# A hybrid encoder layer: attention by kv group with wide moving value products, and half of the out projection between its heads

## The chip, the cores and the metric

The kernel runs on one core of a Trainium2 chip. The metric is the device time of one execution in microseconds (us); lower is better. The engines of the core work side by side, each through its own list of instructions in order, and wait for one another by semaphores: TensorE (PE in the profile) multiplies, VectorE (DVE), ScalarE (ACT) and GpSimd (POOL) do the rest, and SyncE (SP) issues most transfers.

## The reference

One layer is applied to two sequences with shared weights, 1024 and 256 tokens, of width 1024. Cut to what matters:

```
h = rms_norm(x); q, k, v, z, xbc, dt, mq = split(h @ w_in)
q = rope(rms_norm(q))                       # 16 heads of 64
k = rope(rms_norm(k))                       # 4 kv heads, each shared by 4 query heads
for each block of 128 queries, with its 3 neighbouring key blocks:
    sc = q k^T * scale, masked to |i - j| <= 128 and to the sequence
    m = max(max(sc), sink); p = exp(sc - m); denom = sum(p) + exp(sink - m)
    attn = (p / denom) @ v
ssm_out = bidirectional state-space scan; mem_out = attention to 256 memory tokens
x = x + concat(attn, ssm_out, mem_out) @ w_out      # 2048 x 1024
x = x + W_down(silu(conv(gate)) * conv(up)),  [gate, up] = rms_norm(x) @ w_up
```

All is float32. Where precision allows, the kernel splits an operand into a high part in a reduced form (F32R) and a low rest, and multiplies in two or three passes.

## The kernel before

The 1280 tokens are 10 tiles of 128 (`NT`): 8 of the long sequence (`TP`) and 2 of the short. The stages follow one another, each a block with its own buffers and semaphores: norm, input projections, ssm, `attention`, `memory`, `out_projection`, `ffn`. Between stages the data lies in DRAM: `proj` holds the projections, `mix_t` the concatenated outputs, turned, a tile at a time as 128 x (16 x 128).

**`attention`** first prepares all keys (norm, rotary, turned into `kt_hi` and `kt_lo`, with zero blocks at the ends of each sequence), and then loops over tiles and in each over 16 heads (`tile`). A head takes two score products over 384 columns (L969, L970) into `s_ps`, a custom VectorE operation that masks, scales and takes the maximum (L887, `at_sm`, `at_nm`), the exponential on ScalarE (L752, `at_pr`), three turns of the weights on TensorE (L943, `at_tps`), a VectorE copy (L867, `at_pt`), and the value product (L955), in which a block of 128 weights is the stationary operand and 64 value columns are the moving one, in float32:

```python
for k in range(3):
    m = T.matmul(o_ps[:, h], pt[:, h % 2, k], rhs, start=(k == 0), stop=(k == 2))
```

The steps of a head are spread over the slots of the next heads: turns two heads late, values four. Queries of the next tile are prepared on GpSimd in operations of 128 x 1024 (L672 to L686), `high` on ScalarE (L716) stands in head 4 and the turns (`q_unit`, L922) in heads 10 to 13, into two banks of `x_ps` by turns, evacuated by ScalarE (L720). The outputs are divided by the denominator (L852), turned (`o_unit`, L935) and stored.

**`memory`** is the same kind of attention over 256 memory tokens.

**`out_projection`** multiplies `mix_t` by the 16 row chunks of `w_out` in two parts, of 10 and 6 chunks, since not all split weights fit beside the result: the first part for all tiles, then the second, each adding into `x1` in SBUF. A chunk is three products of 512 columns for each half of the width. Loads of the mix go from ScalarE's queue. In the second part each tile is also normed, turned (`turn`) and split into `h_hi` and `h_lo` for the ffn. Lines: splits of the weights on VectorE L2028 and L2030, of the mix L1975 (ScalarE) and L2042 (VectorE), products L2141 and L2120.

**`ffn`** holds `x1` in SBUF and adds to it.

In every stage the order of work on each engine is written out by hand.

## Time and profile before

| | |
|---|---|
| device time, 3 runs | 2328.8, 2332.81 (median), 2338.07 us |
| span of the profiled execution, first to last instruction | 2327.3 us |
| own time of that execution beside its span | not recorded; the median of the runs is 5.5 us above the span |
| attention, first transfer to the next stage's first | 710.5 to 1022.4 us |
| memory | 1022.4 to 1119.8 us |
| out projection | 1119.8 to 1374.8 us |
| ffn | 1374.8 us to the end |

The profile is one execution, recorded by the hardware. Durations of matmuls overlap with those of the next (their ends are modelled), so how fast TensorE works is read from the distance between the starts of two instructions. `[x <-y]` behind a row is the idle time of the engine before it, and what ended it. `x4` is a row in which four like instructions are merged.

### The profile page before, as it was taken

To read this page: it belongs to the slowest core of one execution; us is meant where nothing else is said; L and a number is where in the kernel's file an instruction comes from. 1 tells how busy PE (TensorE), PEld (TensorE's weight loads), DVE (VectorE), ACT (ScalarE), POOL (GpSimd) and SP (SyncE) were. 2 spreads that over 40 slices of the span, in tenths; PEclk is the share of its full clock that TensorE was granted. 3 is DMA by queue.
4 is the path that set the end of the run, shared out by engine and by line. 5 is a ranking of instruction groups with operands and counts; after the bars stand their busy time and mean duration, and the time that the engine had idled before them with its cause. 6 is when DMAs were issued, how large, how long until landed. Compare 5 with 4: busy or idle time off the path is not lost. (4 is left out here: it accounts for less than half of the span.)

```text
span 2327.3 us, 30823 instructions
## 1 busy us (share of the span) xinstructions
PE 2098.8 (90%) x10912; PEld 1759.7 (76%) x10912; DVE 1366.6 (59%) x1843; ACT 609.6 (26%) x1163; POOL 295.5 (13%) x239
## 2 busy tenths in 40 slices
PE   4999999987862899958699979999999999999997
PEld 3887888865652888957578868888888888888885
DVE  6562211116976788857432545667667576676766
ACT  5111111103652656635110322211212112111110
POOL 2000000003654655413000000000000000000000
PEclk7999999999985999979899989999999999999998
DMA  5322222223212111111541121110101101001002
GB/s 169 106 82 84 83 85 87 97 81 105 73 50 101 35 44 43 43 72 60 192 153 43 41 64 45 49 34 27 54 27 33 48 27 54 27 27 54 27 9 90
DMA packets 109191, 152.57 MB, mean 66 GB/s; under 512 B 8512, under 2 KB 68928, under 8 KB 109120
## 3 DMA queue, kind: packets, MB, share of 16 engines
q1 hardware_dynamic: 82784, 109.74, 15.1%
q10 hardware_dynamic: 26336, 41.89, 5.1%
q8 instruction: 44, 0.72, 0.1%
q14 instruction: 27, 0.22, 0.0%
HBM read 115.43 MB, written 36.18 MB: 65 GB/s over the span
## 5 line engine op out<-in xcount | busy, mean ns | idle before, releaser
L2350 DVE TENSOR_TENSOR x<-x,ff_proj 128x512 f32<-128x512 f32 x264 | 181.5, 688 | 190.5 <-PE ff_proj L2411 188.3
L2391 PE MATMUL ff_proj<-h_hi,ff_uhi 128*128 128x512 f32 (+1 forms) x1056 | 264.3, 358 | 10.4 <-DVE ff_ulo L2304 10.4
L2391 PE MATMUL ff_proj<-h_lo,ff_uhi 128*128 128x512 f32 (+1 forms) x1056 | 263.6, 358 | 0.0
L2391 PE MATMUL ff_proj<-h_hi,ff_ulo 128*128 128x512 f32 (+1 forms) x1056 | 263.3, 358 | 0.0
L2391 PEld LDWEIGHTS ff_proj<-h_hi,ff_uhi 128*128 128x128 f32 x1056 | 177.2, 188 | 43.1 <-DVE ff_ulo L2304 10.8
L2391 PEld LDWEIGHTS ff_proj<-h_lo,ff_uhi 128*128 128x128 f32 x1056 | 175.5, 188 | 31.2
L2391 PEld LDWEIGHTS ff_proj<-h_hi,ff_ulo 128*128 128x128 f32 x1056 | 175.5, 188 | 31.3
L416 PE MATMUL pj_bank<-pj_whi,act_hi 128*128 128x512 f32 x464 | 180.7, 390 | 0.0
L416 PE MATMUL pj_bank<-pj_whi,act_lo 128*128 128x512 f32 x464 | 180.5, 389 | 0.0
L416 PE MATMUL pj_bank<-pj_wlo,act_hi 128*128 128x512 f32 x464 | 180.5, 389 | 0.0
L327 DVE CAST pj_whi<-pj_raw 128x1024 fp32r<-128x1024 f32 x36 | 24.9, 692 | 206.1 <-PE pj_bank L416 179.2
L955 PEld LDWEIGHTS at_ops<-at_v,at_pt 128*128 128x128 f32 x960 | 127.3, 191 | 19.9 <-DVE at_pt L867 19.5
L2262 ACT ACTIVATE ff_padded<-ff_proj 128x1024 f32<-128x1024 f32 x44 | 45.3, 1029 | 361.7 <-PE ff_proj L2391 361.7
L955 PE MATMUL at_ops<-at_v,at_pt 128*128 (+1 forms) x960 | 127.0, 268 | 12.0 <-DVE at_pt L867 11.9
L2274 ACT ACTIVATE ff_ahi<-ff_gate 128x1281 fp32r<-128x1281 f32 x22 | 28.1, 1276 | 381.0 <-DVE ff_gate L2339 381.0
L2350 DVE TENSOR_TENSOR x<-x,ff_sums 128x512 f32<-128x512 f32 x176 | 121.0, 688 | 2.8 <-PE ff_sums L2411 0.8
L752 ACT ACTIVATE at_pr<-at_sm,at_nm 128x384 f32<-128x384 f32 x160 | 98.1, 613 | 85.3 <-DVE at_nm L887 76.6
L2411 PE MATMUL ff_proj<-ff_dhi,ff_ahi 128*128 128x512 f32 x264 | 105.2, 398 | 9.2 <-DVE ff_alo L2341 9.2
L887 DVE CUSTOM_DVE_ANT_0 at_sm<-at_sps,at_mask,at_nsink 128x384 f32<-128x384 f32 x160 | 98.0, 613 | 20.8 <-PE at_sps L970 12.9
L500 ACT ACTIVATE pj_stage<-pj_bank 128x512 f32<-128x512 f32 x58 | 34.7, 598 | 277.5 <-PE pj_bank L416 277.5
L2411 PE MATMUL ff_proj<-ff_dlo,ff_ahi 128*128 128x512 f32 x264 | 104.9, 397 | 0.0
L2411 PE MATMUL ff_proj<-ff_dhi,ff_alo 128*128 128x512 f32 x264 | 104.5, 396 | 0.0
(285 smaller groups left out, 4256.5 us busy)
## 6 DMA issues: line engine op xcount, KB each, us to landing
ff_rawu<-w_up SPq DMA_DIRECT2D x44, 512.0 KB, 5.0
pj_raw<-w_in SPq DMA_DIRECT2D x28, 512.0 KB, 3.9
scratch_proj<-pj_stage ACTq DMA_DIRECT2D x50, 256.0 KB, 2.0
ff_rawd<-w_down SPq DMA_DIRECT2D x22, 512.0 KB, 3.5
wo_raw<-w_out SPq DMA_DIRECT2D x16, 512.0 KB, 4.2
n_x<-tokens SPq DMA_DIRECT2D x14, 512.0 KB, 4.2
wo_mix<-scratch_mix ACTq DMA_DIRECT2D x9, 640.0 KB, 3.8
sb_xc<-scratch_xbc_tiles SPq DMA_DIRECT2D x10, 512.0 KB, 3.3
```

The costliest lines, as they stand in the source:

```text
L327: v.tensor_copy(w_hi[:, s, k], raw[:, q % RAW]).then_inc(w_hi_done, 1)
L416: m = nc.tensor.matmul(out, left(a, k), right(c, k), start=(k == 0 and i == 0), stop=(k == KC - 1 and i == 2))
L500: a.activation(stage[:, s], bank[:, g % BANKS], func).then_inc(copied, 1)
L752: nc.scalar.activation(pr[:, h % 4], sm[:, h % 4], ACT.Exp, bias=nm[:, s, h:h + 1], scale=-1.0, accum_out=rowsum[:, s, h:h + 1]).then_inc( ...
L887: v.tensor_tensor_reduce(out=sm[:, h % 4], in0=s_ps[:, h % 2, 0:WIN], in1=mask[:, s], scale=-(DH ** -0.5), scalar=nsink[:, h:h + 1], op0=A ...
L955: m = T.matmul(o_ps[:, h], pt[:, h % 2, k], rhs, start=(k == 0), stop=(k == 2))
L2262: nc.scalar.activation(padded[:, 1:1 + SEQ], proj[:, g, 0:SEQ], ACT.Copy)
L2274: nc.scalar.activation(a_hi[:, 1:GAP + 1 + DEC], gate[:, 1:GAP + 1 + DEC], ACT.Copy).then_inc(a_hi_done, 1)
L2350: nc.vector.tensor_tensor(v, v, ring(g), ALU.add).then_inc(added, 1)
L2391: m = nc.tensor.matmul(proj[:, g, t0:t0 + n], U[w][:, s, k, g], X[x][:, k, t0:t0 + n], start=(k == 0 and r == 0), stop=(k == KC - 1 and r ...
L2411: m = nc.tensor.matmul(ring(g), a[:, c0:c0 + P], w[:, s, cols], start=(r == 0), stop=(r == 2))
```

## The change

`memory` now runs before `attention`, and `attention` does half of the out projection.

**Order of attention.** The loop runs over the 4 kv groups, in each over the 10 tiles, and in each tile over the group's 4 heads (`slots()`, 160 slots; a unit `u` is a tile of a group). The keys of a group are prepared one group ahead on GpSimd (`keys`), in buffers of two groups, without zero blocks: `blocks(t)` gives the 2 or 3 key blocks that exist, so a tile at an end of a sequence has 256 score columns. Queries are prepared by pairs of tiles, 4 heads each (128 x 512), and turned in two goes, `query_turn(v, 0)` and `(v, 1)`. All turns but those of the weights go through one bank, `x_ps`, in an order that `x_order()` lists.

**Value products.** Values are split and doubled, `v_two` holds a block as [high, low] side by side: 128 columns, the stationary operand. The moving operand is the turned weights of all 4 heads, 512 columns, themselves split into `p_hi` (ScalarE) and `p_lo` (VectorE). So the result is turned already, but has a high and a low half of 64 partitions each, which are stored apart in `mix_t` and `mix_b` and added later, and isn't yet divided: the reciprocals go to DRAM (`rec`), and the next stage multiplies by them.

**Half of the out projection.** Chunks 8 to 15 of `w_out` (the ssm and memory rows) are split in the start of `attention`; tile 0 is multiplied there, and the other 144 chunks one in each slot (`fill`), with the residual added and stored to `part`. The stage `out_projection` does chunks 0 to 7, starting from `part`; a tile's mix is two loads, eight small broadcast loads of the reciprocals, an addition on GpSimd (`whole`) and a multiplication on VectorE (`weigh`). `x1` goes through DRAM and the ffn loads it.

The diff, cut to its core (`...` where lines are left out). TensorE's loop in `attention`:

```diff
+            def rest_of_part():
+
+                for q in range(2, TILE_GROUPS):
+                    n, c = divmod(q, 2)
+                    pe.wait_ge(m_split, n + 1)
+                    pe.wait_ge(added, q - 1)
+                    for k in range(CH):
+                        chunk(n, c, k)
+                        yield
...
+            def x_free(n):
+
+                if n > 0:
+                    pe.wait_ge(S["xcopy"], n)
...
+            def query_turn(v, i):
+                x_free(use_no[("q", v, i)])
+                pe.wait_ge(S["qlo"], v + 1)
+                for h in range(QG):
+                    o = T.transpose(x_ps[:, h], q_two[:, i, h].rearrange("p a d -> p (a d)"), ident[:, :])
+                o.then_inc(S["x"], 1)
...
+            def output(u, x):
...
+                w = v_two[:, g % 2, ks[x]].rearrange("p a d -> p (a d)")
+                T.matmul(o_ps[:, :], w, p_hi[:, c % 2], start=(x == 0), stop=False)
+                T.matmul(o_ps[:, :], w, p_lo[:, c % 2], start=False, stop=(x == len(ks) - 1)).then_inc(S["o"], 1)
...
+            fill = rest_of_part()
+            for u, g, t, h, v in slots():
+                scores(u, g, t, h, v)
+                if h > 0 and u > 0 and h - 1 < len(blocks((u - 1) % NT)):
+                    probs_turn(u - 1, h - 1)
+                if t % 2 == 1 and h < 2 and v + 1 < HKV * PAIRS:
+                    query_turn(v + 1, h)
+                next(fill, None)
+                if h == 3 and u > 0:
+                    output(u - 1, 0)
+                if h < 2 and u > 1 and h + 1 < len(blocks((u - 2) % NT)):
+                    output(u - 2, h + 1)
+                if (t, h) in K_TURN and g + 1 < HKV:
+                    key_turn(g + 1, K_TURN[t, h])
```

ScalarE's and VectorE's loops, and GpSimd's last query step:

```diff
+            for u, g, t, h, v in slots():
+                i, n = t % 2, split_due(QG * u + h)
+                probs(u, h)
+                if h > 0 and u > 0 and h - 1 < len(blocks((u - 1) % NT)):
+                    probs_high(turns_before(u - 1) + h - 1)
+                if n is not None:
+                    mix_high(n)
+                if i == 1 and h == 2 and v + 2 < HKV * PAIRS:
+                    square(v + 2)
+                if i == 0 and h == 3 and v + 1 < HKV * PAIRS:
+                    high(v + 1)
+                if i == 1 and h in (1, 2) and v + 1 < HKV * PAIRS:
+                    query_evac(v + 1, h - 1)
...
+            for u, g, t, h, v in slots():
+                k = QG * u + h
+                scores(u, g, t, h)
+                if h >= 2 and u > 0:
+                    probs_low(turns_before(u - 1) + h - 2)
...
+                if h == 2 and u >= 2:
+                    out_evac(u - 2)
+                n, q = split_due(k), evac_due(k)
+                if n is not None:
+                    mix_low(n)
+                if q is not None and q >= 2:
+                    add(q)
...
+            def queries_low(v):
+                pool.wait_ge(S["qhi"], v + 1)
+                g_.tensor_tensor(q_two[:, :, :, 1].bitcast(F32R), q_c[:, :, :, :], q_two[:, :, :, 0],
+                                 ALU.subtract).then_inc(S["qlo"], 1)
```

`out_projection`, SP's loads and the order of VectorE:

```diff
+            def mixed(t):
+                if t > 0:
+
+                    sp.wait_ge(m_split, t)
+                sp.dma_start(mix[:, :, :], mix_t[t][:, 0:CH * P]).then_inc(mix_loaded, 16)
+                sp.dma_start(mix2[:, :, :], mix_b[t]).then_inc(mix_loaded, 16)
+                for e in range(2):
+                    for g in range(HKV):
+                        sp.dma_start(rec[e * DH:(e + 1) * DH, 2 * g:2 * g + 2],
+                                     rec_v[t, e, g].unsqueeze(0).broadcast_to([DH, 2, P])).then_inc(mix_loaded, 16)
...
+            for t in range(2, NT):
+                mixed(t)
+                store(t - 2)
+                residual(t)
...
+            for t in range(2, NT):
+                weigh(t)
+                add(t - 2)
+                low(t)
+                if t >= 3:
+                    norm(t - 3)
+                    turned(t - 3)
```

The ffn:

```diff
+            load(1)
+            sp.dma_start(y[:, :, :], x1_dram.rearrange("(t p) d -> p t d", p=P)).then_inc(y_loaded, 16)
```

## Rows read from the trace of the kernel before

**Rows 1.** The page: span, and busy time of each engine.
```profile
span 2327.3 us, 30823 instructions
...
PE 2098.8 (90%) x10912; PEld 1759.7 (76%) x10912; DVE 1366.6 (59%) x1843; ACT 609.6 (26%) x1163; POOL 295.5 (13%) x239
```

**Rows 2.** Stretches: us, busy time of engines, PEclk, DMA share, GB/s.
```profile
710.50:758.90 48.40, 9.76 (x57) 8.32 (x57) 34.57 (x36) 14.35 (x20) 30.74 (x15) 0.58 0.32 110
758.90:1013.00 254.10, 238.22 (x1942) 227.23 (x1943) 218.85 (x560) 154.21 (x408) 127.78 (x70) 1.00 0.12 40
1013.00:1022.40 9.40, 5.24 (x44) 4.62 (x43) 3.44 (x10) 2.48 (x7) 0.00 (x0) 0.90 0.14 56
1022.40:1119.80 97.40, 65.37 (x416) 55.30 (x416) 57.31 (x106) 39.82 (x116) 30.34 (x36) 0.85 0.24 78
1119.80:1374.80 255.00, 232.46 (x1040) 190.41 (x1040) 109.08 (x102) 42.98 (x50) 7.46 (x22) 0.96 0.28 95
1119.80:1163.90 44.10, 31.40 (x120) 23.79 (x120) 24.61 (x24) 3.82 (x3) 0.13 (x2) 0.81 0.68 231
```

**Rows 3.** Order of time, head loop: start, us, engine, line, operation.
```profile
847.21 0.60 ACT L752 ACTIVATE at_pr<-at_sm,at_nm 128x384 f32<-128x384 f32 x1
...
847.81 0.60 ACT L752 ACTIVATE at_pr<-at_sm,at_nm 128x384 f32<-128x384 f32 x1
...
848.69 0.42 PE L969 MATMUL at_sps<-at_kthi,at_qt 128*128 x1
...
849.14 0.78 PE L955 MATMUL at_ops<-at_v,at_pt 128*128 x6
849.53 0.62 DVE L887 CUSTOM_DVE_ANT_0 at_sm<-at_sps,at_mask,at_nsink 128x384 f32<-128x384 f32 x1 [0.43 <-PE at_sps L970]
...
849.75 0.50 PE L943 MATMUL at_tps<-at_ident,at_pr 128*128 128x128 f32 x3
...
850.01 0.42 PE L969 MATMUL at_sps<-at_kthi,at_qt 128*128 x1
...
850.07 2.33 DVE L861 TENSOR_TENSOR at_t<-at_nm,at_sink 128x8 f32<-128x8 f32 x1
...
850.19 0.62 ACT L752 ACTIVATE at_pr<-at_sm,at_nm 128x384 f32<-128x384 f32 x1 [0.58 <-DVE at_nm L887]
```

**Rows 4.** Order of time: handovers of queries; in brackets the idle time before.
```profile
757.73 1.09 ACT L720 ACTIVATE at_qt<-at_xps 128x512 fp32r<-128x512 f32 x2 [0.26 <-PE at_xps L922]
...
758.87 0.45 PE L969 MATMUL at_sps<-at_kthi,at_qt 128*128 128x384 f32 x1 [0.69 <-ACT at_qt L720]
...
846.25 1.06 ACT L716 ACTIVATE at_qtwo<-at_qn 128x1024 fp32r<-128x1024 f32 x1 [1.63 <-POOL at_qn L683]
...
847.38 2.37 POOL L686 TENSOR_TENSOR at_qtwo<-at_qn,at_qtwo 128x1024 fp32r<-128x1024 f32 x1 [1.25 <-ACT at_qtwo L716]
```

**Rows 5.** Out projection: two products in order of time; a group of VectorE.
```profile
1164.51 0.39 PE L2120 MATMUL wo_bank<-h_hi,wo_mlo 128*128 128x512 f32 x1
...
1164.74 0.39 PE L2120 MATMUL wo_bank<-h_hi,wo_mhi 128*128 128x512 f32 x1
...
L2030 DVE TENSOR_TENSOR h_lo<-wo_raw,h_hi 128x1024 fp32r<-128x1024 f32 x10 | 12.2, 1224 | 0.3
```

**Rows 6.** The ssm stage: products behind two idle times; a stretch at the second.
```profile
577.54 1.98 PE L1628 MATMUL sf_dps<-sf_atri,sf_ones 128*128 128x512 f32 x4 [2.39 <-POOL sf_atri L1680]
...
644.44 3.28 PE L1628 MATMUL sf_dps<-sf_atri,sf_ones 128*128 128x512 f32 x4 [1.90 <-POOL sf_atri L1680]
...
644.00:650.00 6.00, 5.56 (x20) 3.54 (x20) 5.87 (x5) 3.02 (x6) 4.22 (x4) 0.72 0.51 175
```

**Rows 7.** DMA: two issues on SP's queue; issues by line, KB each, us to landing.
```profile
714.07 0.91 SPq L629 DMA_DIRECT2D at_wrow<-k_norm_w  x2
...
wo_raw<-w_out SPq DMA_DIRECT2D x16, 512.0 KB, 4.2
...
scratch_mix<-me_ot ACTq DMA_DIRECT2D x10, 256.0 KB, 2.1
```

More of the change, by code:

```diff
@@ L903, in _ @@
+            sink_term(HKV - 1)
+            if len(blocks(NT - 2)) > 2:
+                probs_low(turns_before(UNITS - 2) + 2)
+            for x in range(len(blocks(NT - 1))):
+                probs_low(turns_before(UNITS - 1) + x)
+            out_evac(UNITS - 2)
+            invert(HKV - 1)
+            out_evac(UNITS - 1)
         @block.tensor
@@ L996, in memory @@
+            for _ in fill:
+                pass
+            x1 = UNITS - 1
+            output(x1 - 1, 1)
+            if len(blocks((x1 - 1) % NT)) > 2:
+                output(x1 - 1, 2)
+            for x in range(len(blocks(NT - 1))):
+                probs_turn(x1, x)
+            for x in range(len(blocks(NT - 1))):
+                output(x1, x)
+            sums_turn(HKV - 1)
 def memory(nc, proj, mem_proj, ident_dram, small, mix_t):
@@ L1954, in _ @@
+            for t in (NT - 2, NT - 1):
+                store(t)
+            for s in range(3):
+                sp.wait_ge(x_stored[s], 16 * len(range(s, NT, 3)))
         @block.gpsimd
@@ L1968, in _ @@
+            for t in range(NT):
+                whole(t)
+                if t >= 3:
+                    inverse(t - 3)
+            for t in range(NT - 3, NT):
+                inverse(t)
         @block.scalar
         def _(act):
-            def high(n, s, count):
-                act.wait_ge(mix_loaded, 16 * n + 16)
-                if not (isinstance(n, int) and n < 2):
-                    act.wait_ge(multiplied, n - 1)
-                nc.scalar.activation(m_hi[:, s, 0:count], mix[:, 0:count], ACT.Copy).then_inc(m_hi_done, 1)
@@ L2083, in _ @@
-            for t in range(CHUNKS[1], NT):
-                add(t, t, t % 2)
-                low(t + 2, t % 2, int(t + 2 >= NT))
-            dve.wait_ge(added, NT)
-            dve.wait_ge(const_loaded, 32)
-            def step(u, s):
-                if not (isinstance(u, int) and u in (0, NT - 1)):
-                    low(NT + u + 1, 1 - s, 1)
-                if not (isinstance(u, int) and u < 1):
-                    norm(u - 1)
-                if not (isinstance(u, int) and u < 2):
-                    turned(u - 2)
-                add(NT + u, u, s)
@@ L2100, in _ @@
+            add(NT - 2)
+            norm(NT - 3)
+            turned(NT - 3)
+            add(NT - 1)
+            norm(NT - 2)
             turned(NT - 2)
@@ L2105, in _ @@
         def _(pe):
[L2106 to L2122 removed]
+            T = nc.tensor
@@ L2124, in turn, with chunk @@
+            def chunk(t, c, k):
+                s = t % 2
+                for i, (l, r) in enumerate(((m_hi, w_hi), (m_hi, w_lo), (m_lo, w_hi))):
+                    m = T.matmul(bank[:, s, c], l[:, s, k], r[:, k, c * PW:(c + 1) * PW],
+                                 start=(k == 0 and i == 0), stop=(k == CH - 1 and i == 2))
+                return m
             def turn(t):
                 pe.wait_ge(normed, t + 1)
-                if not (isinstance(t, int) and t == 0):
+                if t > 0:
@@ L2143, in _ @@
-                    if k == CHUNKS[0] - 1:
+                        m = chunk(t, c, kk)
+                    if kk == CH - 1:
                         m.then_inc(multiplied, 1)
-            with pe.Fori(1, NT // 2) as j:
-                for s in range(2):
-                    tile(0, 2 * j + s, s)
-            pe.wait_ge(w_split, 2 * KC)
             pe.wait_ge(const_loaded, 32)
-            def step(u, s):
-                if not (isinstance(u, int) and u < 2):
-                    turn(u - 2)
-                tile(1, NT + u, s)
@@ L2156, in _ @@
-            second_part(pe, step)
-            turn(NT - 2)
-            turn(NT - 1)
-def ffn(nc, hi, lo, w_up, w_down, conv_w, conv_b, y, out):
+            for t in range(2, NT):
+                pe.wait_ge(m_split, t + 1)
+                pe.wait_ge(added, t - 1)
+                for c in range(2):
+                    for k in range(CH):
+                        m = chunk(t, c, k)
+                        if c == 0 and k == 3 and t >= 3:
+                            turn(t - 3)
+                m.then_inc(multiplied, 1)
@@ L2165, in ffn @@
+            for t in range(NT - 3, NT):
+                turn(t)
+def ffn(nc, hi, lo, w_up, w_down, conv_w, conv_b, x1_dram, out):
     PAD = TOK + 3
```

1134 lines of the change are left out of this document (622 added, 512 removed).

## The prediction, made before the changed kernel ran

> **What bounds the kernel now.** I read the page first: TensorE is busy nine tenths of a span of 2327.3 us [rows 1]. The median of the runs shown, 2332.81 us, lies 5.5 us above that span, so I sum against the span and add 5.5. Then the table by stretches [rows 2]. Attention runs from 710.5 to 1022.4 (311.9 us): 48.4 us of start in which TensorE hardly works, 254.1 us of head loop with 238 us busy, 9.4 us of tail. Memory takes 97.4, the out projection 255.0, of which 44.1 is a start filled by transfers. The ffn behind it is touched only by a later load. Busy times count overlap, so for work I take distances between starts. In the head loop [rows 3] a head's two score products take 0.45 us (848.69 to 849.14), its value products 0.61 (to 849.75), its three turns of the weights 0.26 (to 850.01): 0.087 us a turn. With 24 other turns per 16 heads (0.13) that is 1.45 us of a slot of 254.1/160 = 1.59. So TensorE bounds this loop, with 0.14 us a slot to spare: work put between the heads is not free, it lengthens the loop nearly by itself. In the out projection a 128x512 product follows the last after 0.23 us (1164.51 to 1164.74) [rows 5], and nothing else bounds the loop.
>
> **What is taken away.** The value products (160 x 0.61 = 98 us) become 104 key blocks x 2 products of 512 columns x 0.23 = 48 us. Blocks fall from 480 to 416 quarter turns, and the 80 turns of the outputs go.
>
> **The new loop by TensorE's work.** Scores: 160 x 0.39 (0.45 at three blocks, about 0.11 less at two, which are 4 tiles in 10, and a little less where a wide product hides the weight load) = 62. Weights turned: 416 x 0.087 = 36. Queries and keys: 182 x 0.087 = 16. Values: 48. Out projection between the heads: 144 chunks x 3 x 0.23 = 99. A wide product behind turns loads its weights in the open, 0.09 by estimate (the score pair's 0.45 is more than the value pass of the same columns would need): 9. Sum 270 us, against 254.1. VectorE does 0.49 for the scores (0.54 at three blocks, 849.53 to 850.07 [rows 3]), 0.40 for `probs_low` (half of 1.22 for half the size [rows 5], 0.65 a slot), 0.15 for the outputs and 0.2 for the rest, 1.24 us a slot; ScalarE does 0.55, 0.34 and 0.35 in the same way. Both stay under TensorE's 1.7. GpSimd has seven half-size query operations in each pair of tiles, at 1.2 at most [rows 4], some 8 us of 13.
>
> **Two waits are added in each pair of tiles.** This is where I expect the change to lose, for TensorE executes in order, and what stands behind a waiting turn (the chunk of the out projection above all) waits with it.
>
> First, `query_turn(v + 1, 0)` stands in slot 0 of the odd tile. It waits for `queries_low`, which waits for `high(v + 1)`, which stands on ScalarE behind the exponential of slot 3 of the even tile. From the start of that slot's scores [rows 3, 4]: scores to VectorE 0.84 (848.69 to 849.53), to the exponential 0.66 (850.19), 0.60 until ScalarE is free (847.21 to 847.81), `probs_high` 0.52 (half of 1.09, less overlap), `high` 0.60 (between half and all of 1.06, for half the size), 0.07 of handing over, GpSimd 1.19 (half of 2.37), 0.06: 4.54 us. TensorE arrives after scores 0.45, turn 0.35, chunk 0.78, values 0.46 and scores 0.45, that is after 2.5, or 0.2 less since VectorE reaches slot 3 late (it copies an output in slot 2). Stall: 2.2 us.
>
> Second, `query_turn(v + 1, 1)` in slot 1 needs the only `x_ps` bank back, whose evacuation stands on ScalarE behind slot 1's exponential and `probs_high`: 0.84 + 0.66 + 0.60 + 0.52 + 0.55 + 0.05 = 3.2 us after that slot's scores, while TensorE is there after 0.45 + 0.35 = 0.8. Stall: 2.4 us.
>
> Together 4.6 us x 19 pairs = 88 us. Before, `q_unit` had two banks and ran 5 slots behind its `high`, and in this loop's rows TensorE goes on without a pause [rows 3]. Lower bound 0 (only if TensorE came 2 us late by itself), upper 5.5 (VectorE another 0.5 late each time).
>
> Eight tiles also split a mix tile in slot 2: ScalarE ends `mix_high` (1.06, the size of `high` before [rows 4]) 3.7 us after that slot's scores, VectorE ends `mix_low` 1.22 later [rows 5], and scores of slot 3 wait until 4.9 where they would be ready at 2.4. That delays the first wait by 2.5: 20 us, between 0 and 25.
>
> **The clock.** While TensorE idled 2.39 us in the ssm stage, its next four products took 1.98 us; after an idle 1.90 us in another tile they took 3.28, with a granted clock of 0.72 in that stretch [rows 6]. So a gap of this length sometimes brings the 1.2 GHz level, for a price of 1.3 to 1.8 us. Each pair now has two such gaps with 2 us of work between. I take half of the 19 pairs at 1.6: 15 us; bounds 0 and 19 x 4 = 76. The Trainium skill ("TensorE: Matmul & The Clock Gate", section "HAM oscillation") says that a kernel whose bursts are split by waits falls to the lower clock before every burst. By that rule every pair would pay; the traced gap of 2.39 us did not.
>
> **Start and tail of attention.** The start had 48.4 us. The constants' loads are the same; the key chain on GpSimd and then the queries take about as long as before, but VectorE now splits eight weight chunks, each two loads apart: two buffers give (4.2 + 1.9)/2 = 3.05 us a chunk [rows 5, 7], done at 40, then three key turns in one bank (5 us), two query turns, mix and two adds: 52. The tail grows from 9.4 to 12 by two output copies and eight stores. Bounds 45 and 62.
>
> Attention: 52 + 270 + 88 + 20 + 15 + 12 = 457, that is +145. Memory only moves: 0.
>
> **The out projection.** Half of the products leave: 480 x 0.23 = 110 us less on TensorE. But the stage stops being bound by it. A tile's mix has one buffer: the next load may go only when `low` is done. From there: the norm step and store, 1.25; ten transfers on SP at 0.46 each (0.91 for two) 4.6, and 2.1 for the last to land, as for a small store [rows 7]; on GpSimd `whole` 2.4, the size of its operation in [rows 4]; `weigh` 1.22, `mix_high` 1.06, `low` 1.22 [rows 4, 5], handovers 0.3. That is 14.1 us a tile, against 48 x 0.23 + 0.8 = 11.8 for TensorE. The lower bound is these 11.8; the upper 17, if 512-byte pieces land slower. The Trainium skill's fit for one transfer ("SBUF — State Buffer", section "The DMA setup-cost knee": about 2 us plus bytes at 436 GB/s) would give 5.6 us for the 1.5 MB at once, and a tile of 13; the row beside it, 512 KB in 4.2 us [rows 7] where the fit says 3.2, makes me keep 14.1.
>
> The start moves 4 MB of weights, three mixes of 1.5 MB and two residuals, at the 231 GB/s of the old start [rows 2] 41 us, plus the last mix's way through three engines, 6, and waits in SP's order: 51 until tile 2. Then 7 x 14.1 = 99, the last tile 12, and a tail of 16 (three tiles are still to be turned and scaled, each 0.8 + 1.22 + 1.06 + 1.22 = 4.3, and 3 for adds and norms): 178 against 255.0, that is -77. The ffn's load of x1 (5 MB, about 20 us) lies under its first two projections (some 60 us); uncovered it would cost 20. I take 0.
>
> **Sum.** 2327.3 + 145 - 77 = 2395.3, plus 5.5 = 2401 us.
>
> **The rivals.**
> - The turns cost nothing (faster). The place is the two `query_turn` in each pair. If TensorE were late by 2 us at each for reasons of its own, the 88, the 20 and the 15 go: 2278 us. It decides from 55 us in all on, that is about 2.1 us a pair where I have 4.6. For it: before, this loop ran with hardly a gap. Against it: both chains start at a score product that TensorE itself issued only 0.8 and 2.5 us earlier, and no step of them can overlap. Chance 0.12.
> - The clock falls in every pair (the rule above): 15 becomes about 55: 2441 us. Chance 0.15.
> - The second stage is bound by TensorE after all, 11.8 a tile: 16 us less, and 6 off the start: 2379. For it: rates near 400 GB/s are possible where pieces are large; against it: eight of ten transfers carry 64 KB. Chance 0.13.
> - VectorE and GpSimd get in each other's way. An addition of 128x8 took 2.33 us at 850.07 [rows 3]; if the splits in the start and the mix pay 1 us each, and the eight waits with them: +25, 2426. Chance 0.10.
> - The forecast, 2365 to 2430: chance 0.50.
>
> **The numbers.** Only the first rival ends under 2333, so faster by over 0.5% (a shift under about 12 us cannot be told from none here) has 0.11, within 0.5% 0.04, slower 0.85. The range 2335 to 2445 leaves out most of the first rival and a part of the second.
>
> **What would show it.** In attention: TensorE idle before the turns of `at_qtwo` into `at_xps`, about 2.2 and 2.4 us, 19 times each, released by GpSimd's `at_qtwo` and ScalarE's `at_qt`; a loop near 390 us; granted clock under 1.00. In the out projection: products in bursts of 11 us, 14 us apart, released by `wo_mlo`, GpSimd's `wo_mix` behind the loads. I am wrong if the loop takes under 300 us, or if the attention stage grows by less than the out projection shrinks.

## The result: 5% slower, 2448 us

The changed kernel takes 2448.23 us (median of 4 runs, 2447.38 to 2454.06), the kernel before 2335.44 beside it: a ratio of 1.0502, 95% interval 1.0481 to 1.0523. The forecast was slower, 2401 us, with a range to 2445: the sign and the places are as foretold, the size is short by 47 us, and the time lies 3 us above the range. The profiled execution has a span of 2445.6 us against 2327.3 [rows 1]. In spans the miss is 50 us (2445.6 for 2395.3), and this is what the stages below add up to: the forecast added 5.5 us for the median over the span, and it is 2.6 here.

The page after, span and busy time of each engine:

```profile
span 2445.6 us, 28665 instructions
...
PE 2086.1 (85%) x10020; PEld 1710.6 (70%) x10020; DVE 1331.6 (54%) x1776; ACT 647.4 (26%) x1265; POOL 379.5 (16%) x371
```

TensorE is busy for 12.7 us less than before [rows 1] in a span that is 118.3 us longer, so its idle time has grown by 131 us. The table by stretches says where (columns as in [rows 2]); the rows are the start of attention, its head loop, its tail, and then start, tiles and tail of the out projection:

```profile
809.30:868.90 59.60, 21.87 (x66) 14.88 (x67) 30.51 (x29) 7.22 (x11) 36.03 (x28) 0.64 0.51 148
868.90:1279.00 410.10, 309.98 (x1556) 254.80 (x1555) 214.50 (x529) 210.78 (x531) 176.49 (x178) 0.89 0.28 73
1279.00:1289.00 10.00, 1.83 (x11) 1.12 (x8) 3.09 (x6) 1.48 (x4) 0.00 (x0) 0.76 0.34 72
1289.00:1346.50 57.50, 28.02 (x96) 21.32 (x96) 21.84 (x21) 2.11 (x2) 7.15 (x5) 0.71 0.57 175
1346.50:1476.00 129.50, 105.93 (x448) 84.82 (x448) 51.11 (x48) 26.00 (x33) 29.80 (x25) 0.91 0.48 154
1476.00:1493.50 17.50, 3.94 (x16) 3.14 (x16) 9.82 (x9) 4.22 (x5) 0.74 (x2) 0.58 0.07 30
```

Attention takes 479.7 us (809.3 to 1289.0) for 311.9, the out projection 204.5 for 255.0; memory takes 98.0 for 97.4 and the ffn behind them is as long as before. The loop is idle for 100 us and its clock is 0.89, where it was idle for 16 at 1.00 [rows 2]; 1.00 is the level of 2.4 GHz throughout, 0.89 a mix of it with 1.2 GHz.

The largest waits of TensorE from 868 to 1290 us, the loop and its edges (released by, us in total, times, longest):

```profile
PE at_xps L1160 <- POOL at_qtwo L838: 58.8, 19, 4.4
PE at_xps L1160 <- ACT at_qt L900: 33.2, 20, 2.0
```

These are the two waits that the forecast added. One of the 20 (0.7 us) stands just ahead of the loop; the others, 19 of each, are 91.3 us of the loop's 100. In order of time one pair of them looks so (start, us, operation, idle time before it with its releaser):

```profile
965.90 0.28 PE L1178 MATMUL at_sps<-at_kthi,at_qt 128*128 128x256 f32 x1
966.02 0.28 PE L1179 MATMUL at_sps<-at_ktlo,at_qt 128*128 128x256 f32 x1
968.30 0.63 PE L1160 MATMUL at_xps<-at_ident,at_qtwo 128*128 128x128 f32 x4 [1.99 <-POOL at_qtwo L838]
968.68 0.48 PE L1125 MATMUL wp_bank<-wp_hi,wp_mhi 128*128 128x512 f32 x1
969.00 0.40 PE L1125 MATMUL wp_bank<-wp_lo,wp_mhi 128*128 128x512 f32 x1
969.23 0.39 PE L1125 MATMUL wp_bank<-wp_hi,wp_mlo 128*128 128x512 f32 x1
969.46 0.40 PE L1202 MATMUL at_ops<-at_phi,at_vtwo 128*128 128x512 f32 x1
...
969.93 0.28 PE L1178 MATMUL at_sps<-at_kthi,at_qt 128*128 128x256 f32 x1
...
970.16 0.60 PE L1189 MATMUL at_tps<-at_ident,at_pr 128*128 128x128 f32 x4
972.51 0.66 PE L1160 MATMUL at_xps<-at_ident,at_qtwo 128*128 128x128 f32 x4 [1.75 <-ACT at_qt L900]
```

TensorE gives out the scores at 965.90, comes to the first query turn and stands 2 us; it then has the turn, a chunk (three products), value products, the next scores and turns of the weights to do, 1.9 us in all, and stands again for 1.75. None of what is issued behind the turn shows a wait of its own; whether it could have run meanwhile is tried below for the chunk.

The first wait comes in two sizes: 4.0 to 4.4 us in the eight pairs with a split of the mix, 1.9 to 2.7 in the other eleven (one of 1.99 is shown above). And the clock falls in some pairs only. The pair shown above, and one whose first wait was 4.3 us (columns as in [rows 2]):

```profile
966.30:984.30 18.00, 12.51 (x73) 10.40 (x72) 9.46 (x25) 9.32 (x24) 8.08 (x8) 1.00 0.41 92
1024.70:1042.70 18.00, 12.12 (x49) 10.00 (x49) 7.34 (x18) 7.10 (x18) 6.78 (x7) 0.72 0.11 30
```

Read in steps of 1 us, the granted clock is below 1.00 at some time in 15 of the 19 pairs, in all eight of the long waits and in seven of the others.

### The profile page after: what moved, and what is told of

The parts are those of the page before. It is cut to its first block and busy times, and to the rows that moved or that the text cites. A ratio compares the mean times of both kernels' runs of the same rounds, so it can differ in the third digit from the quotient of the medians.

```text
span 2445.6 us, 28665 instructions
## 1 busy us (share of the span) xinstructions
PE 2086.1 (85%) x10020; PEld 1710.6 (70%) x10020; DVE 1331.6 (54%) x1776; ACT 647.4 (26%) x1265; POOL 379.5 (16%) x371
## 5 line engine op out<-in xcount | busy, mean ns | idle before, releaser
L1030 DVE CUSTOM_DVE_ANT_0 at_sm<-at_sps,at_mask,at_nsink 128x384 f32<-128x384 f32 (+1 forms) x160 | 89.7, 561 | 170.5 <-PE at_sps L1179 169.4
L921 ACT ACTIVATE at_pr<-at_sm,at_nm 128x384 f32<-128x384 f32 (+1 forms) x160 | 91.5, 572 | 195.8 <-DVE at_nm L1030 195.0
L327 DVE CAST pj_whi<-pj_raw 128x1024 fp32r<-128x1024 f32 x36 | 24.9, 692 | 206.8 <-PE pj_bank L416 177.6
L2344 PE MATMUL wo_bank<-wo_hi,wo_mhi 128*128 128x512 f32 x160 | 70.1, 438 | 59.0 <-DVE wo_mlo L2288 49.1
L1125 PE MATMUL wp_bank<-wp_hi,wp_mhi 128*128 128x512 f32 x160 | 79.8, 499 | 40.7 <-DVE wp_lo L1008 37.6
L1160 PE MATMUL at_xps<-at_ident,at_qtwo 128*128 128x128 f32 x160 | 30.7, 323 | 93.0 <-POOL at_qtwo L838 58.8
```

What stands on the lines that cost most here:

```text
L921: a.activation(pr[:, n % 8, 0:w], sm[:, n % 2, 0:w], ACT.Exp, bias=nm[:, n:n + 1], scale=-1.0, accum_out=rowsum[:, n:n + 1]).then_inc(S["e ...
L1030: v_.tensor_tensor_reduce(out=sm[:, n % 2, 0:w], in0=s_ps[:, n % 2, 0:w], in1=mask[:, mask_at(t):mask_at(t) + w], scale=-(DH ** -0.5), sca ...
L1125: m = T.matmul(bank[:, c], l[:, n % 2, k], r[:, k, c * PW:(c + 1) * PW], start=(k == 0 and i == 0), stop=(k == CH - 1 and i == 2))
L1160: o = T.transpose(x_ps[:, h], q_two[:, i, h].rearrange("p a d -> p (a d)"), ident[:, :])
L2344: m = T.matmul(bank[:, s, c], l[:, s, k], r[:, k, c * PW:(c + 1) * PW], start=(k == 0 and i == 0), stop=(k == CH - 1 and i == 2))
```

## The experiments

Each run is an edit of the changed kernel, and all compute the whole reference. "Loop" is from the first to the last score product (406.5 us in the changed kernel). A median is that of 4 to 6 runs, a ratio that to the kernel before, run on the same chip.

| run | us | ratio, 95% | loop us | clock, busy in loop | out projection us |
|---|---|---|---|---|---|
| changed kernel | 2448.2 | 1.048 to 1.052 | 406.5 | 0.89, 308 | 204.2 |
| turns apart | 2384.0 | 1.022 to 1.025 | 338.2 | 0.98, 282 | 206.8 |
| high half early | 2410.3 | 1.033 to 1.037 | 366.5 | 0.93, 296 | 207.1 |
| chunk ahead of turn | 2405.1 | 1.030 to 1.033 | 363.8 | 0.94, 292 | 206.3 |
| two reciprocal loads | 2455.3 | 1.050 to 1.056 | 405.9 | | 210.9 |
| mix split in slot 0 | 2455.6 | 1.049 to 1.056 | 412.8 | 0.88, 316 | 206.6 |
| four loop edits | 2349.2 | 1.005 to 1.009 | 307.6 | 0.96, 280 | 206.0 |
| mix loads early | 2418.4 | 1.033 to 1.039 | 406.3 | | 176.0 |
| start split | 2446.8 | 1.045 to 1.053 | 407.8 | | 207.3 |
| all together | 2314.6 | 0.991 to 0.994 | 305.3 | 0.97, 277 | 173.4 |
| and mix in halves | 2310.9 | 0.990 to 0.993 | 302.9 | 0.98, 276 | 174.9 |
| all, mix's low half later | 2301.6 | 0.985 to 0.990 | 290.0 | 0.98, 274 | 173.1 |

The out projection is measured from the issue of its first load to the end of the last `h_lo`; between equal stages it varies by 3 us. TensorE's products in the loop are the same in all these runs.

**The turns apart.** In TensorE's and ScalarE's slots:

```diff
-                if t % 2 == 1 and h < 2 and v + 1 < HKV * PAIRS:
-                    query_turn(v + 1, h)
+                if t % 2 == 1 and h in (1, 3) and v + 1 < HKV * PAIRS:
+                    query_turn(v + 1, h // 2)
...
-                if i == 1 and h in (1, 2) and v + 1 < HKV * PAIRS:
-                    query_evac(v + 1, h - 1)
+                if i == 1 and h == 2 and v + 1 < HKV * PAIRS:
+                    query_evac(v + 1, 0)
+                if i == 0 and h == 0 and u > 0:
+                    query_evac(v, 1)
```

> The two query turns of an odd tile go from slots 0 and 1 to slots 1 and 3, their evacuations to slot 2 and to slot 0 of the next tile; nothing else changes. If the added waits hold the head loop (410 us in the changed kernel), the first turn comes a slot later to a result that is ready at the same time (its stall 3.1 becomes about 1.2 us) and the second finds its bank long free (1.7 becomes 0): 19 x 3.6 = 68 us, the loop about 342, the whole about 2380. If TensorE would have been late by itself, or VectorE sets the pace of the slots (TensorE's stalls only taking the place of its waits for scores), the loop stays within 10 us of 410 and the whole near 2445.

The loop is 68.3 us shorter, the whole 64. The waits of this run:

```profile
PE at_xps L1162 <- ACT at_qt L900: 19.8, 19, 1.5
PE at_xps L1162 <- POOL at_qtwo L838: 14.3, 18, 1.6
```

The first stall fell further than expected (58.8 to 14.3 us in all), the second less (32.5 in the loop to 19.8, not to 0: its chain through ScalarE is longer than the one slot between evacuation and turn). The sum of the two is 57. Some 15 us of it came back as other waits (9.3 us before value products, 4.5 before key turns), so TensorE's idle time in the loop fell by 42, from 98 to 56; the other 26 of the 68 us are busy time, 282 us for 308 at a clock of 0.98 for 0.89. So about a quarter of the waiting at the turns would have been waited elsewhere without them, and not all of it, as the first rival had it.

**The high half early.** On ScalarE:

```diff
+                if i == 0 and h == 2 and v + 1 < HKV * PAIRS:
+                    high(v + 1)
                 if n is not None:
                     mix_high(n)
...
-                if i == 0 and h == 3 and v + 1 < HKV * PAIRS:
-                    high(v + 1)
```

> ScalarE makes the high half of the next queries in slot 2 of the even tile, ahead of the split of the mix, not in slot 3 behind its exponential; the turns stay in slots 0 and 1. By the theory of the waits the first stall goes from 3.1 to 0.3 us (the low half is ready 4.5 us after slot 2's scores, TensorE comes 4.2 after them), the second stays at 1.7: 19 x 2.8 = 53 us, the loop about 357, the whole about 2395; of it 8 x 2.5 = 20 us is the mix, which stands behind now. If the stall only moves (GpSimd is late for its own reasons, or slot 3's exponential is now late by 0.6), the whole stays above 2430.

Of this run's waits at the turns (868 to 1290 us):

```profile
PE at_xps L1160 <- ACT at_qt L900: 36.0, 20, 2.2
...
PE at_xps L1160 <- DVE at_ktlo L995: 10.7, 3, 4.5
PE at_xps L1160 <- POOL at_qtwo L838: 8.0, 13, 0.9
PE at_xps L1160 <- ACT at_rect L906: 5.6, 3, 3.9
```

GpSimd's wait goes from 58.8 to 8.0 us, 0.6 a time (0.3 was expected), but the loop gives back 40 and not 53. A turn that no longer waits for its data now waits in six tiles for its bank, which a key turn or the turn of the sums holds (10.7 and 5.6 us): one bank for three kinds of turn is a wait behind the wait.

**The chunk ahead of the turn.** On TensorE:

```diff
+                next(fill, None)
                 if t % 2 == 1 and h < 2 and v + 1 < HKV * PAIRS:
                     query_turn(v + 1, h)
-                next(fill, None)
```

> In the slots with a query turn the chunk of the out projection (three products of 512 columns, 0.7 us) is issued ahead of the turn, not behind it. If a wait costs what TensorE has nothing to put under it, each of the two stalls shrinks by the chunk: 19 x 2 x 0.7 = 26 us, the loop about 384, the whole about 2422. If the loop's length is set by the chain of scores, exponential and query preparation that runs beside TensorE, the chunk fills idle time but nothing ends sooner: the whole at 2440 or more.

The waits at the turns fall from 91.3 to 64.6 us in the loop, 26.7 as expected, yet the loop is 42.7 us shorter. The difference stands in the busy time: 292 us for the same products that took 308, at a clock of 0.94 for 0.89. So the clock makes a microsecond of waiting cost about 1.6 here (42.7/26.7); the forecast had 15 us of clock on 108 of waits, 1.14. By the idle time of the whole loop the price is 1.6 in the run with the turns apart too, 1.5 with the high half early, and 1.4 over the whole way from the changed kernel to the last run (116.5 us of loop for 82.7 of idle time).

**The mix split in slot 0.**

```diff
-            n, r = divmod(k + 22, 16)
+            n, r = divmod(k + 24, 16)
```

> The split of each of the eight mix tiles goes from slot 2 to slot 0 of the same even tile; turns and high halves stay as in the changed kernel. By the forecast's third term the split stands in the chain to the first query turn with 2.5 us, 8 times: 20 us less, the loop about 390 (410 now), the whole about 2428. If the split costs the same wherever it stands (it holds ScalarE for 1.05 and VectorE for 1.22 us), the loop stays at 405 or more and the whole above 2440.

```profile
PE at_xps L1160 <- POOL at_qtwo L838: 33.0, 15, 2.5
```

From 860 to 1200 us this wait has 33.0 us in 15 times, 2.2 each; in the changed kernel it has 51.4 us in 16 times, 3.2 each. So the chain did get shorter by 1.0 us a pair, and over the whole loop the first wait is 42.2 us for 58.8: no stall of 4 us is left. But the loop is 6.3 us longer. TensorE is idle for 97 us as before (98), for new waits before value products, turns of the weights and key turns have taken the place of the old, and its products take 8 us more. The split costs as much where it stands now. My reason for the term (it lies in the chain to the query turn) holds where the split stood; it was wrong as a reason to expect a gain by moving it.

**Four edits of the loop.** The three edits above in one kernel (turns apart, high half early, chunk ahead), and:

```diff
                 i, n = t % 2, split_due(QG * u + h)
+                if i == 1 and h == 2 and v + 1 < HKV * PAIRS:
+                    query_evac(v + 1, 0)
+                if i == 0 and h == 0 and u > 0:
+                    query_evac(v, 1)
                 probs(u, h)
```

> The edits of the first three runs together (turns in slots 1 and 3, the high half in slot 2 of the even tile, the chunk ahead of a turn), and ScalarE's evacuation of a query turn ahead of its exponential. In the run with the turns apart 34 us of stalls at the query turns were left (14.3 and 19.8) at a granted clock of 0.98. If the waits are all that the change costs the loop, these go too and the clock with them: a loop of about 302 to 305, the whole about 2346, TensorE's busy time about 278 us. If TensorE's work in the loop is larger than the 270 us of the forecast, or VectorE sets the pace of the slots from here on, the loop stays above 320 and the whole above 2362.

The loop is 307.6 us, 98.9 less. No wait at a query turn is left in it. The largest that is left is this:

```profile
PE at_ops L1204 <- DVE at_plo L1039: 19.4, 11, 4.7
```

**Two reciprocal loads.** The row order of `rec_dram` becomes (tile, e, g, c), by a permuted reciprocal and two stores; then:

```diff
                 for e in range(2):
-                    for g in range(HKV):
-                        sp.dma_start(rec[e * DH:(e + 1) * DH, 2 * g:2 * g + 2],
-                                     rec_v[t, e, g].unsqueeze(0).broadcast_to([DH, 2, P])).then_inc(mix_loaded, 16)
+                    sp.dma_start(rec[e * DH:(e + 1) * DH, :, :],
+                                 rec_v[t, e].unsqueeze(0).broadcast_to([DH, CH, P])).then_inc(mix_loaded, 16)
```

> The reciprocals of the sums are stored so that a tile of the out projection loads them with two transfers of 256 KB, not eight of 64 KB; bytes and arithmetic are the same. If the issue of ten transfers at 0.65 us is what makes a tile 17 us long, six issues less give 3.9 us a tile, 13.1, so 7 x 3.9 = 27 us and some 4 more in the stage's start: the whole about 2417. If the bytes (1.5 MB a tile) or the way to memory take the time, the last transfer lands when it did: 2445.

The time is 2455, not 2417: the number of issues was not what made a tile long. In order of time, a tile of the changed kernel, from VectorE's `low` to GpSimd's next `whole`:

```profile
1364.62 1.23 DVE L2288 TENSOR_TENSOR wo_mlo<-wo_mix,wo_mhi 128x1024 fp32r<-128x1024 f32 x1
1364.66 0.33 SPq L2191 DMA_DIRECT2D scratch_x<-wo_x  x1
...
1366.60 0.33 SPq L2187 DMA_DIRECT2D wo_x<-scratch_part  x1
...
1366.97 0.43 SPq L2173 DMA_DIRECT2D wo_mix<-scratch_mix  x1
...
1367.91 5.16 SPq L2177 DMA_DIRECT2D wo_rec<-scratch_rec  x8
...
1375.45 2.39 POOL L2222 TENSOR_TENSOR wo_mix<-wo_mix,wo_mixb 128x1024 f32<-128x1024 f32 x1 [11.54 <-DMA wo_rec<-scratch_rec]
```

And of this run, from the mix's request:

```profile
1369.09 0.43 SPq L2176 DMA_DIRECT2D wo_mix<-scratch_mix  x1
...
1370.04 1.15 SPq L2179 DMA_DIRECT2D wo_rec<-scratch_rec  x2
...
1377.88 2.39 POOL L2224 TENSOR_TENSOR wo_mix<-wo_mix,wo_mixb 128x1024 f32<-128x1024 f32 x1 [11.84 <-DMA wo_rec<-scratch_rec]
```

The reciprocals' issues take 1.15 us, where they took 5.16, and `whole` starts 8.8 us after the mix's request, for 8.5. The last landing is 6.7 us behind the last issue now, and was 2.4: the requests go sooner and the data come no sooner. (In the six tiles from this one on, `whole` comes 8.5 to 9.9 us after the mix's request in the changed kernel and 8.8 to 10.4 in this run.) What both have in common is the sum: store, residual, mix, second part and reciprocals are five times 512 KB, requested within 9 us, and the last has landed 10.8 us after the store's issue (1364.66 to 1375.45). That is about 240 GB/s, near the 231 of the stretch that the transfers filled before [rows 2].

**The mix loads early.** On top of the two loads; SP asks for each part as soon as its buffer has been read, the second part and the reciprocals ahead of the store, the mix ahead of the residual:

```diff
             for t in range(2, NT):
-                mixed(t)
+                if t + 1 < NT:
+                    others(t + 1)   # second part: waits for summed; reciprocals: wait for weighed
                 store(t - 2)
+                if t + 1 < NT:
+                    mixed(t + 1)    # waits for m_split
                 residual(t)
```

> Two reciprocal transfers a tile as in the run before (2455 us), and the next tile's second mix part and reciprocals are requested as soon as GpSimd's sum and VectorE's product have read the old ones, ahead of the store and the residual's load, instead of behind both. Theory that replaces mine: after each tile's low half, five transfers (2.6 MB: store, residual, mix, second part, reciprocals) go at once and take 11 us at about 240 GB/s, and it is this, not the issue, that makes the tile 16 to 17 us; with 1 MB requested 3 to 4 us earlier a tile takes about 13, the stage 25 us less than in the run before: the whole about 2428. If the time is in the landing of one transfer (7.4 us for 256 KB of reciprocals) and not in the sum of bytes, the reciprocals land before the mix does and the tile falls further, to TensorE's 11.8: 2418. If the early transfers only delay the mix, nothing changes: 2450.

```profile
1356.01 0.32 SPq L2181 DMA_DIRECT2D wo_mixb<-scratch_mixb  x1
...
1357.27 1.09 SPq L2185 DMA_DIRECT2D wo_rec<-scratch_rec  x2
...
1359.62 0.34 SPq L2176 DMA_DIRECT2D wo_mix<-scratch_mix  x1
...
1364.88 2.40 POOL L2237 TENSOR_TENSOR wo_mix<-wo_mix,wo_mixb 128x1024 f32<-128x1024 f32 x1 [7.22 <-DMA wo_mix<-scratch_mix]
```

`whole` now starts 5.3 us after the mix's request, and is released by the mix itself and no longer by the reciprocals. The tiles come 12.4 us apart (seven of them in 87.1, for 16.3 and 114.0 in the changed kernel), 0.6 above the 11.8 that the forecast had for TensorE, and the stage takes 176.0 us, the whole 2418. That is the number of the other reading in the expectation, the time of one transfer, and not the 2428 worked out from the sum of bytes, so the time alone does not choose between them. The landing times do. Median us from issue to landing in the out projection (512 KB each, the reciprocals 256 KB):

| run | store | residual | mix | second part | reciprocals |
|---|---|---|---|---|---|
| two reciprocal loads | 2.6 | 4.1 | 5.3 | 6.4 | 7.4 |
| mix loads early | 5.2 | 6.9 | 6.3 | 3.2 | 4.6 |

The same transfer takes twice as long or half, by what was requested ahead of it: 7.4 us is not the time of a reciprocal load as such. So the transfers in flight delay each other; which of the store, the residual and the reciprocals delays the mix most was not separated.

**The start split.** ScalarE gets `w_hi`, and the second `reduce` stands behind chunk 4:

```diff
-                dve.wait_ge(w_loaded[k % 2], 16 * (k // 2 + 1))
-                v_.tensor_copy(w_hi[:, k], raw[:, k % 2]).then_inc(w_hi_done, 1)
                 dve.wait_ge(w_hi_done, k + 1)
...
-                if k == 2:
+                if k == 4:
                     reduce(1)
```

> In the start of attention ScalarE makes the high parts of the eight weight chunks (VectorE only the low parts), and VectorE's reduction of the second query pair stands behind the fifth chunk, not the third, where it waited 2.9 us for GpSimd. If VectorE and GpSimd in each other's way (high parts of 0.68 us taking up to 1.77, low parts of 1.22 up to 2.46) and that wait make the start 59.6 us long where 52 was forecast, it becomes about 53, the whole about 2441. If the arrival of the weights sets it (two buffers), it stays at 58 or more, 2447.

The start is 54.8 us, 4.8 less; in the median (2446.8) that does not show beside the spread. In the changed kernel, VectorE and GpSimd in order of time:

```profile
842.92 0.69 DVE L1002 TENSOR_REDUCE at_qss<-at_qsq 128x8 f32<-128x512 f32 x1 [2.90 <-POOL at_qmse L827]
843.52 0.68 DVE L1006 CAST wp_hi<-wp_raw 128x1024 fp32r<-128x1024 f32 x1
844.24 1.23 DVE L1008 TENSOR_TENSOR wp_lo<-wp_raw,wp_hi 128x1024 fp32r<-128x1024 f32 x1
...
849.27 1.99 POOL L810 TENSOR_TENSOR at_vtwo<-at_vraw,at_vtwo 128x640 fp32r<-128x640 f32 x1
849.89 2.46 DVE L1008 TENSOR_TENSOR wp_lo<-wp_raw,wp_hi 128x1024 fp32r<-128x1024 f32 x1
851.23 2.26 POOL L820 TENSOR_TENSOR at_qc<-at_qraw,at_table 128x512 f32<-128x512 f32 x1
852.27 1.77 DVE L1006 CAST wp_hi<-wp_raw 128x1024 fp32r<-128x1024 f32 x1
```

The high part of a chunk took between 0.68 and 1.77 us, its low part between 1.22 and 2.46. The long ones end a fixed time behind the end of a GpSimd operation: the low part of 849.89 ends at 852.35, 1.1 us after GpSimd's at 851.26, and the high part of 852.27 at 854.04, 0.55 us after GpSimd's next at 853.49, as if each had begun only then. The Trainium skill ("SBUF — State Buffer", section "SBUF: two separate sides") says that GpSimd shares a pair of ports with VectorE operations in a two-port mode or with two inputs in SBUF, and that one instruction holds it to its end while the other is blocked; these rows agree. All sixteen operations took 22.6 us, where 0.68 and 1.22 each would give 15.2. The forecast's sum had nothing for it in the start, only its fourth rival. The run does not separate how much of the 4.8 us is this, how much the 2.9 us that VectorE stood before 842.92 (for GpSimd's reading of `at_qss`), and how much the high parts that VectorE no longer makes at all.

**All together.**

> The four edits of the head loop, the start split over ScalarE and VectorE, and the two reciprocal transfers requested early, in one kernel. If the three causes are separate, their gains add: stage by stage 99 us in the loop, 5 in the start, 33 in the out projection, less 2 of spread, so 2448 - 135 = 2313, which is 0.8% under the kernel before. If they were one cause seen three times (a lower clock over the whole, or transfers that collide again), less than the sum is left: over 2330.

2314.6 us, against a sum of 2313: the gains add, as those of separate causes do. The loop's largest wait is still the one before value products:

```profile
PE at_ops L1216 <- DVE at_plo L1050: 19.6, 12, 4.8
```

Eight of its twelve are of 1.8 to 4.8 us, and each stands in a slot with a mix split. One of them, VectorE's and ScalarE's side:

```profile
1020.99 1.05 ACT L938 ACTIVATE wp_mhi<-wp_mix 128x1024 fp32r<-128x1024 f32 x1
...
1022.07 1.47 DVE L1026 TENSOR_TENSOR wp_mlo<-wp_mix,wp_mhi 128x1024 fp32r<-128x1024 f32 x1 [1.42 <-ACT wp_mhi L938]
...
1023.46 0.47 DVE L1043 CUSTOM_DVE_ANT_0 at_sm<-at_sps,at_mask,at_nsink 128x256 f32<-128x256 f32 x1
...
1023.87 0.68 DVE L1050 TENSOR_TENSOR at_plo<-at_tps,at_phi 128x512 fp32r<-128x512 f32 x1
...
1024.60 0.50 PE L1216 MATMUL at_ops<-at_phi,at_vtwo 128*128 128x512 f32 x1 [2.20 <-DVE at_plo L1050]
```

VectorE stands 1.4 us for `mix_high`, splits for 1.5, and only then comes to scores that were ready; `at_plo` behind them is what TensorE waits for.

**The mix in halves.** `mix_high` and `mix_low` for four of the eight chunks at a time, the second half in slot 3:

```diff
-                if n is not None:
-                    mix_low(n)
+                for z in range(2):
+                    n = split_due(QG * u + h - z)
+                    if n is not None:
+                        mix_low(n, z)
```

> As the run before, with the split of each mix tile made in two halves in two slots (four operations of about 0.55 and 0.65 us in place of two of 1.05 and 1.22). In the loop with all four edits, 19.4 us of TensorE's waits stand before value products, released by VectorE's low half of the weights, 11 times with 4.7 us as the longest; if these are the mix's splits in VectorE's way, halves that fit into a slot's idle time take some 10 of them: about 2303. If they have another cause, the time stays within 4 us of the run before, or rises by the fixed cost of 32 more operations.

2310.9, within 4 us of the run before, the time that the expectation's other reading gave. The wait is still 17.8 us: VectorE still stands for ScalarE, only for less at a time (0.6 to 1.2 us at most halves, where it stood 1.4 to 1.5 once).

**The mix's low half later.** All together, and one line:

```diff
-                n, q = split_due(k), evac_due(k)
+                n, q = split_due(k - 1), evac_due(k)
```

> As the run of all edits together (2315 us), with VectorE's low half of each mix tile one slot later, behind that slot's scores and weights, so that VectorE no longer stands 1.4 us waiting for ScalarE's high half with the next scores behind it. The eight waits of about 2 us (one of 4.7) ahead of value products stand in just the slots of the mix splits. If VectorE's wait in order is what they are, they shrink by 1.4 us each and more where the clock fell: 10 to 14 us, the loop about 293, the whole about 2303, and the third term of the forecast (20 us) is then a matter of this one order. If it is the work of the split that TensorE waits for (2.3 us of ScalarE and VectorE), wherever it stands, at most 4 us go: 2311 or more.

2301.6 us, 1.25% under the kernel before (ratio 0.9854 to 0.9896). The loop, by waits and as a stretch:

```profile
PE at_ops L1216 <- DVE at_plo L1050: 1.0, 4, 0.3
```

```profile
865.00:1155.00 290.00, 274.40 (x1547) 229.88 (x1545) 213.13 (x523) 208.04 (x527) 185.01 (x178) 0.98 0.39 104
```

The wait before value products is 1.0 us, for 19.6. In its place TensorE waits 5.8 us more for exponentials (7.7 for 1.9); idle time and products together make the loop 15.3 us shorter. Of the time that the mix still cost here, most was VectorE waiting in order for a result of ScalarE in the same slot.

## Why the prediction came out short

**What held.** Both added waits stand where the forecast put them, with the releasers and the counts that it named, and TensorE's work in the loop is right: forecast 270 us, measured 274 at a clock of 0.98 in the last run. The first stall was foretold at 2.2 us, and at 4.7 in the eight tiles with the mix in its chain; it is 2.3 and 4.2 on average. The second is 1.7 for 2.4. Together with the 20 us of the mix the forecast has 108 us of waits; the loop is idle for 98. Memory (98.0 for 97.4), the tail (10.0 for 12) and the ffn (0) are within 2 us.

**The step that failed in the loop is the clock's price.** "I take half of the 19 pairs at 1.6: 15 us." The loop was to take 393 us (270, 88, 20 and 15) and takes 410. The 406.5 us to the last score product are 274 us of work, 98 of idle time and 34 of slower products: busy time is 308 with the waits and 274 without most of them, product for product, and times the granted clock (0.89 and 0.98) the two are nearly the same, 274 and 269. The clock's term is 34 us, twice the 15 and between that and the 55 of the rival in which it falls in every pair. That this rival's total, 2441, is so near what was measured is chance: its loop would be 433 us, and the rest of the miss lies elsewhere. Both factors of the term were too small: 15 pairs fell to the lower clock and not 9 or 10, and they paid 2.3 us each on average (34/15) and not 1.6. The Trainium skill ("TensorE: Matmul & The Clock Gate", section "HAM oscillation") describes a kernel with waits of about 3 to 5 us between its bursts, in which every burst starts at the lower clock. That bears on the eight waits of 4.0 to 4.4 us, and there the trace agrees, with a lower clock in every such pair; the forecast's second rival took it for a rule of all 19. Of the eleven pairs with shorter waits four kept the clock at 1.00: in the pair shown above the chunk behind a stall of 2 us runs at 0.23 us a product, the distance of full speed [rows 5], so that pair paid nothing. What decides among the shorter ones stays open. That the loop's total came within 17 us is in part luck: the waits were 10 us too many and the clock 19 too few.

**The out projection is the larger miss: 204.5 us for 178.** "Ten transfers on SP at 0.46 each (0.91 for two) 4.6, and 2.1 for the last to land" is the term: 6.7 us, where 8.5 to 9.9 were measured in six tiles and 10.9 in the one before them. An issue of the reciprocals took 0.65 us and not 0.46 (eight in 5.16), but the run with two loads shows that this was not what counted. The failed step is the overlap: the forecast took the landing of one small store [rows 7] for a transfer with 2 MB of others in front. A tile was 16.3 us and not 14.1 (15 us in seven tiles), the start 57.5 and not 51, the last tile and the tail 5 more. (Some 2 of the start's 6 us are a slip of units: its 9.5 MB are 9.96 million bytes, and these at 231 GB/s take 43 us and not 41.) It was in the rows: a stretch that transfers filled ran at 231 GB/s [rows 2], and five transfers of 512 KB at that rate are 11 us. I had used that row for the stage's start and not for its tiles, and the store and the residual, which go in the same moment, were in no sum.

**The start of attention, 59.6 for 52.** The splits were to be done 40 us into the stage, at 3.05 a chunk, and were done at 49.8 (859.1), at 3.7 a chunk from 829.1 on; what follows them was 2 us shorter than forecast. The forecast costed the splits by their loads and by durations of VectorE alone, with GpSimd at work beside it. They took 7.4 us more than those durations, and VectorE stood 2.9 us for the misplaced reduction. The run with the start split gets 4.8 us back, in part by taking work off VectorE; how the 9.8 divide among these causes stays open.

**The term of the mix** (20 us) was near: the eight stalls with it are 1.9 us longer than the other eleven, 16 us in all. What the forecast did not see is that the split costs as much two slots off the chain to the query turn (run with slot 0). With the turns out of the way it falls by 15 us when VectorE no longer waits for ScalarE in the slot.

**The rivals.** That the turns cost nothing is out: with them apart the loop is 68 us shorter, though some 15 us of waits came back elsewhere. A second stage bound by TensorE came nearly true (12.4 us a tile for 11.8) once the loads went early. VectorE and GpSimd in each other's way is seen in the start.

So the change moved 50 us out of the out projection and put 168 into attention. With the order of a few instructions put right, the reciprocals in two loads and the splits of the start shared with ScalarE, the same change takes 28 us less than the kernel before (2301.6 beside 2329.7): its idea (wide value products, chunks as fill) was sound, and the slots in which its handovers stand were not.

## What to carry to other kernels

Work put between dependent steps fills nothing if the step that waits stands ahead of it in an engine that executes in order: put the fill before the wait, and set each handover at least as many slots apart as its chain through the other engines is long. Count for each wait of TensorE the slower products behind it too; here a microsecond of idle time cost 1.4 to 1.6 in all. For a stage with one buffer a tile, add up the bytes of all transfers that one event releases, the stores among them, and divide by the rate of a stretch that transfers fill, before counting issues; and ask for each part as soon as its own buffer is read.

## What the runs showed of the hardware

- The same products and turns of the loop (1547 in the trace) took 308 us of busy time at a granted clock of 0.89 and 274 at 0.98. The clock recovered with the idle time, though not in step with it: 0.94 with 26 us of idle time less, 0.98 with 42 less, but 0.96 with 70 less, in the run of four loop edits, where waits of up to 4.7 us before value products were left.
- Behind waits of 4.0 to 4.4 us the clock fell in all of eight pairs of waits; where the first wait was 1.9 to 2.7 us, in seven of eleven.
- Eight transfers of 64 KB or two of 256 KB for the same reciprocals made no difference to when the last landed (8.5 and 8.8 us after the mix's request in the tiles shown), though their packets differ: in the out projection's stretch the trace counts 12576 packets under 2 KB with eight, 1376 with two.
- A transfer of 512 KB on SP's queue landed 2.6 to 6.9 us after its issue (medians of store, residual, mix and second part in two runs), by what else was in flight.
- SP's issue of a reciprocal load took 0.65 us, that of a plain one mostly 0.33 to 0.43.
- A VectorE cast of 128x1024 took from 0.68 to 1.77 us while GpSimd worked, a subtraction from 1.22 to 2.46; the long ones end 0.55 and 1.1 us behind the end of a GpSimd operation.
